# A paged-attention decoder step on Trainium2: GpSimd's building of the next sequence's queries in two earlier parts, and two PSUM copies given from VectorE to ScalarE

## What is computed

```
def one(args):
    pages, qn, qp, lat_new, kp_new = args
    lat = jnp.concatenate([cache_lat[layer, pages].reshape(past, KV_LORA), lat_new], axis=0)
    kp = jnp.concatenate([cache_kpe[layer, pages].reshape(past, QK_ROPE), kp_new], axis=0)
    k_nope, v = expand_kv(lat, w_ukv, k_nope_norm)
    return attend(qn, qp, k_nope, kp, v, mask)
o = lax.map(one, (page_table, q_nope, q_pe, latent_new, k_pe_new))
```

## Time and profile before

| what | value |
|---|---|
| time, median of 3 runs | 1579.99 us (1579.91 to 1580.33) |
| the profiled execution's own time | 1581.96 us |
| its span | 1580.0 us |
| PE busy | 1550.8 us, 98% |
| DVE, ACT, POOL busy | 1056.6, 891.5, 524.7 us |
| granted PE clock | full in all slices |
| chain that ended last | PE 81% (line 820 53%, line 1075 20%), DVE 5%, ACT 4%, issue 3%, POOL 2% |
| stretch of sequences 0 to 7, layer 1 and 2 | about 138 to 389 us and 922 to 1173 us |

### The profile page before, as it was taken

One profiled execution on the slowest core, in us unless ns is written; L12 is line 12 of the kernel. 1 busy time (PEld: TensorE's weight loads), 2 busy tenths in 40 slices (PEclk: granted clock), 3 DMA queues, 4 the chain that ended last, 5 costly groups with the idle time before them and its releaser, 6 DMA issues.

```text
span 1580.0 us, 33275 instructions
## 1 busy us (share of the span) xinstructions
PE 1550.8 (98%) x10796; PEld 1507.2 (95%) x10796; DVE 1056.6 (67%) x1620; ACT 891.5 (56%) x1740; POOL 524.7 (33%) x709
## 2 busy tenths in 40 slices
PE   7999999999999999999999999999999999999999
PEld 7987999999999999999998789999999999999999
DVE  6777767776664766664376877777775658666633
ACT  5787776777533444443357877677764335444432
POOL 3723377676600000000048224777766001000000
PEclk9999999999999999999999999999999999999999
DMA  7331454553645444444454224545436444444443
GB/s 277 121 102 51 117 171 145 147 149 104 187 132 156 148 146 149 152 153 146 146 189 130 77 66 118 179 141 153 139 117 178 138 157 147 147 146 148 155 148 113
DMA packets 114722, 224.65 MB, mean 142 GB/s; under 512 B 12881, under 2 KB 78706, under 8 KB 114482
## 3 DMA queue, kind: packets, MB, share of 16 engines
q1 hardware_dynamic: 112178, 214.75, 44.1%
q0 software_dynamic: 2432, 8.49, 1.6%
HBM read 220.73 MB, written 2.46 MB: 141 GB/s over the span
## 4 chain that ended last, share of the span: by engine, by line
PE 81%; DVE 5%; ACT 4%; issue 3%; POOL 2%; POOLq 2%; DVEq 2%; ACTq 1%; DMA 0%; SPq 0%
PE PS L820 53%; PE PS L1075 20%; DVE w_lo L1768 1%; PE PS L1105 1%; PE PS L1106 1%; POOL r_lo L751 1%; ACT w_hi L1321 1%; POOLq L724 1%; DVEq L1762 1%; ACT r_hi L1321 1%; PE PS L876 1%; ACT lt_hi L1321 1%; PE PS L847 1%; POOL q_rot L711 0%; DVEq L2049 0%
## 5 line engine op out<-in xcount | busy, mean ns | idle before, releaser
L1768 DVE TENSOR_TENSOR w_lo<-raw,w_hi 128x1024 fp32r<-128x1024 f32 x258 | 324.9, 1260 | 221.3 <-ACT w_hi L1321 218.4
L1321 ACT ACTIVATE w_hi<-raw 128x1024 fp32r<-128x1024 f32 x258 | 272.2, 1056 | 348.6 <-PE PS L820 334.4
L820 PE MATMUL PS<-h_hi,w_hi 128*128 128x320 f32 x1360 | 425.9, 313 | 11.2 <-DVE h_lo L1795 10.4
L820 PE MATMUL PS<-h_lo,w_hi 128*128 128x320 f32 x1360 | 420.8, 309 | 0.0
L820 PE MATMUL PS<-h_hi,w_lo 128*128 128x320 f32 x1360 | 420.7, 309 | 0.0
L820 PEld LDWEIGHTS PS<-h_hi,w_hi 128*128 128x128 f32 x1360 | 255.9, 188 | 14.6 <-issue 9.6
L820 PEld LDWEIGHTS PS<-h_lo,w_hi 128*128 128x128 f32 x1360 | 256.0, 188 | 1.0
L820 PEld LDWEIGHTS PS<-h_hi,w_lo 128*128 128x128 f32 x1360 | 255.9, 188 | 0.0
L1321 ACT ACTIVATE ksqp<-PS 128x512 f32<-128x512 f32 x256 | 152.6, 596 | 135.4 <-PE PS L1075 131.6
L2109 DVE TENSOR_REDUCE kss<-ksqp 128x8 f32<-128x512 f32 x256 | 173.2, 680 | 80.5 <-ACT ksqp L1321 79.8
L1075 PE MATMUL PS<-comb_hi,lt_hi 128*128 128x288 f32 x1024 | 224.0, 300 | 3.0 <-DVE lt_lo L1771 1.5
(11 more groups left out here) (325 smaller groups left out, 2683.8 us busy)
## 6 DMA issues: line engine op xcount, KB each, us to landing
raw<-in_stream SPq DMA_DIRECT2D x258, 512.0 KB, 3.5
tpage<-in_tcache SPq DMA_DIRECT2D x256, 160.0 KB, 2.3
rrow<-in_rcache SPq DMA_DIRECT2D x256, 128.0 KB, 2.7
x<-in_xT SPq DMA_DIRECT2D x2, 640.0 KB, 7.0
sbias<-in_sbias POOLq DMA_DIRECT2D x2, 640.0 KB, 6.5
out_yT<-x SPq DMA_DIRECT2D x4, 320.0 KB, 2.2
const<-in_consts SPq DMA_DIRECT2D x1, 1090.0 KB
wgate<-in_wgate POOLq DMA_DIRECT2D x2, 512.0 KB, 4.4
```

Of the source, the lines that this page charges most:

```text
L820: done = mm(out, w[:, slot, c], a, start=first and n == 0 and m == 0, stop=last and n == len(pairs) - 1 and m == 2)
L1321: return nc.scalar.activation(out, in_, func, **kw)
L1768: V.tensor_tensor(w_lo[:, s, :], raw[:, s, :], f(w_hi[:, s, :]), ALU.subtract).then_inc(lo_done.sem, 1)
```

## The change

Three edits. On POOL, `queries` is cut into five helpers of the same operations. The absorbed queries are written in chunk 3, behind `rows_lo`, together with the wait for `pk_mm`; the rotary queries in chunk 5. On ACT, `copy_values` comes at p = 2 and `keep` at p = 10. On DVE both are gone from `sequence` (the calls for the last sequences, behind the pages, stay on DVE).

```diff
-            def queries(b, par):
+            def place_high(b, par):
...
+            def place_low(b, par):
...
+            def rope_high(b, par):
...
-                    if c == 6 and not last:
+                    if c == 3 and not last:
                         if not (isinstance(b, int) and b == 0):
                             pool.wait_ge(pk_mm.sem, pk_mm.at(l, b * NPG))
                             pool.sem_inc(waits_passed, 1)
-                        queries(b + 1, 1 - par)
+                        place_high(b + 1, 1 - par)
+                        pool.drain()
+                        place_low(b + 1, 1 - par)
+                    if c == 5 and not last:
+                        rope_high(b + 1, 1 - par)
+                        pool.drain()
+                        rope_low(b + 1, 1 - par)
+                        pool.drain()
+                        rope_mask(b + 1, 1 - par)
...
+        def copy_values(l, b):
+            act.wait_ge(pv_mm.sem, pv_mm.at(l, b * NPG + NPG))
+            A(olat[:], PS[:, 7, 0:ROW], ACT.Copy).then_inc(s_ev.sem, 1)
+
+        def keep(l, b, bank):
+            act.wait_ge(s_oT.sem, s_oT.at(l, b + 1))
+            for k in range(2):
+                last = A(olatT[:, k, :, bass.ds(b * NT, NT)],
+                         PS[:, bank, 192 + 64 * k:256 + 64 * k].rearrange("p (h t) -> p h t", h=H), ACT.Copy)
+            last.then_inc(s_done.sem, 1)
...
+                if not (isinstance(b, int) and b < 3) and p == 2:
+                    copy_values(l, b - 3)
+                if not (isinstance(b, int) and b < 3) and p == 10:
+                    keep(l, b - 3, 5 - par)
...
-                if older and p == 1:
-                    copy_values(l, b - 3)
...
-                if older and p == 9:
-                    keep(l, b - 3, 5 - par)
```

More of the change, by code:

```diff
@@ L700, in queries @@
                     nc.gpsimd.tensor_copy(comb_hi[:, k, :, q0:q0 + 32], src)
[L701 to L706, removed]
+            def place_low(b, par):
+                q0 = 0 if par else 288
                 for k in range(2):
@@ L710, in queries, with rope_parts, rope_low, rope_mask @@
                                             f(comb_hi[:, k, :, q0:q0 + 32]), ALU.subtract)
+            quarter = cst("quarter").rearrange("p (v o) -> p v o", o=1).to_broadcast([128, 4, HT])
+            def rope_parts(b, par):
+                each = q128[:, bass.ds(b, 1), :].to_broadcast([128, 4, HT])
+                return each, *(q_rot[par][:, i].rearrange("p (v c) -> p v c", v=4) for i in range(2))
+            def rope_high(b, par):
+                each, hi_, _ = rope_parts(b, par)
+                nc.gpsimd.tensor_tensor(hi_, each, quarter, ALU.mult)
+            def rope_low(b, par):
+                each, hi_, lo_ = rope_parts(b, par)
                 nc.gpsimd.tensor_tensor(lo_, each, f(hi_), ALU.subtract)
-                pool.drain()
+            def rope_mask(b, par):
+                _, _, lo_ = rope_parts(b, par)
                 nc.gpsimd.tensor_tensor(lo_, f(lo_), quarter, ALU.mult).then_inc(qc.sem, 1)
-            queries(0, 0)
+            place_high(0, 0)
+            rope_high(0, 0)
+            pool.drain()
+            place_low(0, 0)
+            rope_low(0, 0)
+            pool.drain()
+            rope_mask(0, 0)
             def rotary_lo(b, c):
```

## The result

The changed kernel took 1588.81 us in the median (1587.38 to 1589.97), the kernel before 1580.21 us (1579.91 to 1582.53) beside it. The ratio is 1.0049, with a 95% interval of 1.0036 to 1.0062: 8.6 us, half a per cent, slower. The forecast was 1578.6 us, and the upper end of its range 1583.6 us. The profiled execution of the changed kernel took 1588.93 us.

The account below looks back on a forecast made before the run. PE was taken to bound everything, so only its waits counted. Per layer -4.1 + 0.4 + 3.0 = -0.7 us, -1.4 in all, taking the median from 1579.99 to 1578.6 us; range 1574.2 to 1583.6.

Parts of the forecast that it names:

- queries at sequence starts removed: Starts of sequences 3 to 7: PE's waits for late queries and `r_lo` go, -2.7 us a layer.
- `keep` removed, page 12: Before key page 12, sequences 3 to 6: `lt_lo` starts earlier and PE's wait goes, -1.4 us a layer.
- copies on ACT: Before ACT's squares of pages 3 and 11: the copies fit into idle time, nothing on the path.
- absorbed queries in chunk 3: POOL, chunk 3: rows of chunk 4 come later behind key page 10, +0.4 us a layer.
- rotary queries in chunk 5, page 14: POOL, chunk 5: rows of chunk 6 late behind key page 14, 0.6 us in sequences 2 to 6, +3.0 a layer.
- rival (c): Chunks 3 and 4: `r_lo` just before `lt_lo`, key page 8 waits; 5.6 us on top, 1584.2 us; chance 0.14.
- the one collision: POOL, chunk 5: `r_lo` held up, ending at 316.2 instead of 315.62; expected.
- the second: POOL's queue behind chunk 5: another collision of 0.6 us, making page 14's wait up to 1.15 us; not expected.
- both are tied to the same cast on ACT: Argument against the collision at chunks 3 and 4: POOL's and DVE's starts both depend on one ACT cast.

Follow-up runs that it names:

- queries only: The changed kernel with both copies put back on DVE and removed from ACT; 1588.73 us, ratio 1.0051.
- the probabilities are early: First probabilities split ahead of chunk 1's rotary keys on POOL: changed kernel with this 1578.62 us; also with rotary queries back in chunk 6, 1573.54 us.

## Why the prediction was wrong

Its steps one by one, per layer, against layer 1. The measured numbers are differences of steps between the two kernels, as in the table above, added up over the sequences.

| step of the prediction | forecast | measured |
|---|---|---|
| queries at sequence starts removed | -2.7 | -0.91 - 4 x 0.46 = -2.8 |
| `keep` removed, page 12 | -1.4 | -4 x 0.36 = -1.4 |
| copies on ACT | 0 | 0 |
| absorbed queries in chunk 3 | +0.4 | 0 at page 10, 0.4 within the next row |
| rotary queries in chunk 5, page 14 | +3.0 | +4.4 |
| rival (c): the collision at page 8 | not in the sum | +4.1 |
| sum | -0.7 | +4.3 (the stretch: +4.4) |

**Removed.** Both terms were right in place and size at the starts and at page 12. But the prediction took them as independent of each other, and they are not: the copies alone gained nothing (+1.4 us instead of -2.8), since page 12's wait had covered POOL's delay in chunk 6. In the changed kernel they gained nothing either, as page 14 takes back most of it. The same 2.8 us appeared in full (2.9) once the queue of chunk 6 was 1.0 us shorter.

**Rotary queries in chunk 5.** The mechanism was right: `r_lo` of chunk 5 was held up (1.59 us at 316.64), the queue behind it ran almost without idle (0.41 us before the rows of chunk 6, 0.32 in the earlier trace rows), and the rows of chunk 6 came late at page 14. The size was off. The prediction took 0.6 us with the restart, "as the one collision is likely and the second is not". The second did come: the cast of the probabilities at 320.41 took 0.93 us instead of 0.39. The step from page 14 to page 15 grew by 1.07, 1.00, 0.78, 0.81 and 0.78 us in sequences 2 to 6, 4.4 us in the layer. With the rotary part alone it is 3.0 us, the forecast's number; with the absorbed queries in chunk 3 as well ("queries only") it is 3.4 in layer 1, and the copies on ACT bring the last 1.0. They do it by letting PE come earlier: the rows of chunk 6 start 29.8 to 29.9 us behind key page 0 of sequence 5 in all three kernels. The runs with and without the rotary part in chunk 5 differ by 9.6 us, and by 5.1 us when the probabilities are early.

**The collision at page 8.** This is the step that failed: the sum has nothing for it, and it cost 4.1 us in layer 1 and 3.0 in layer 2. Rival (c) had the place, the two instructions and the price of a wait (0.7 us each; it came to 0.5 us in sequence 7 and 0.85 to 0.94 in sequences 3 to 6), and 0.14 as its chance. What weighed against it, "both are tied to the same cast on ACT", was false: `lt_lo` is only tied to that cast when DVE is free, and DVE had not been free since the `lt_lo` of pages 6 and 7. The prediction looked at chunk 3 alone and put the absorbed queries' cost there; the runs show that the cause is earlier, in the very thing that the change removes. The stall at a sequence's start had held PE and ACT back by 0.46 us, and so had kept POOL's probabilities clear of the `lt_lo` of pages 6 and 7. Had the removed stall's shift been followed through the next sequence, (c) would have been the forecast: -0.7 + 4.1 = +3.4 us a layer, and with page 14 in its true size +4.8.

The trace of the kernel before had the sign of it. The 0.7 us of the earlier trace rows, by which rival (c) was priced, is key page 8 of sequence 2, a sequence whose start has no stall. DVE and POOL there, before:

```profile
208.52 1.64 DVE L1771 TENSOR_TENSOR lt_lo<-tpage,lt_hi 128x512 fp32r<-128x512 f32 x1
```

```profile
208.42 1.20 POOL L751 TENSOR_TENSOR r_lo<-rrow,r_hi 128x512 fp32r<-128x512 f32 x1 [0.25 <-issue]
```

The `lt_lo` of pages 6 and 7 takes 1.16 us in that sequence, and the step at page 7 is 2.45 us. After the change sequences 3 to 6 of layer 1 do as sequence 2 had done.

Layer 2 does not repeat layer 1 to the hundredth, and here that decides. The step at page 7 is 2.5 us in its sequences 3 and 5, 2.2 in 7, and 1.82 in 4 and 6, which is most of why it lost 3.3 us and not 4.4. In 4 and 6 DVE is as late as in the others (`lt_lo` of pages 8 and 9 starts 14.67 us behind key page 0), but `r_lo` starts 0.24 and 0.04 us behind it, and `lt_lo` takes 0.69 us. What sets these few hundredths was not tried.

## What to carry to other kernels

A wait that is removed moves everything behind it against every engine that did not take part in it. So what a removed stall is worth is read only after the shift is followed through the queues of a whole period, to the next place where two engines start together within the shift; and two waits on the same chain are not two gains, since one may cover the other. Where a helper engine's queue has an idle place early in the period, moving work up into it can be worth more than what the moved work takes: here it gave 10.2 us, as the queue ran clear of its neighbour at three places, and brought one new overlap. And a wait that one odd period already has, the first or the one without the stall, is worth a look, as it may show what all the others will do.

## What the runs showed of the hardware

- `lt_lo` on DVE and `r_lo` on POOL, each with two inputs in SBUF, do not share: one runs at its own speed and the other is held up. Started 0.11 and 0.05 us behind `r_lo`, `lt_lo` took 1.63 and 1.70 us while `r_lo` took 1.19 and 1.20; started 0.23 us ahead, `lt_lo` took 0.69 and `r_lo` 1.51. The Trainium skill says the same in Trainium Architecture — The Big Picture, section What this means for kernel authors: the port pair of the two is an exclusive lock and not a split of the bandwidth. The trace agrees: 308.11 + 1.70 = 309.81 is 0.55 us behind the end of `r_lo` at 309.26, nearly the whole 0.68 us that `lt_lo` takes alone.
- So the price of an overlap is what is left of the instruction that came first, less 0.14 us in these rows. `lt_lo` started 0.05, 0.11 and 0.57 us behind `r_lo`, with 1.15, 1.08 and 0.63 us of it left, and took 1.01, 0.94 and 0.49 us more than its 0.69. Beside the probabilities at 302.99, with 0.63 us left, it took 0.49 more. The other way round, `r_lo` at 303.51 had 0.46 us of `lt_lo` left before it and took 0.32 us more than its 1.19. Near a tie the loser changes: 0.11 us behind, `lt_lo` was held up; 0.07 us behind it was not, and `r_lo` took 1.81.
- A copy of 128 x 258 from PSUM took 0.39 us on ACT and 0.42 on DVE (at 296.92 in the kernel before).
